# Rotary rows exchanged by transfers inside SBUF instead of products with a permutation matrix

## The reference

```python
def apply_partial_rope(t, cos, sin):
    tf = t.astype(jnp.float32)
    r1, r2 = jnp.split(tf[..., :ROPE_DIM], 2, axis=-1)      # ROPE_DIM = 16
    rot = jnp.concatenate([r1 * cos - r2 * sin, r2 * cos + r1 * sin], axis=-1)
    return jnp.concatenate([rot, tf[..., ROPE_DIM:]], axis=-1).astype(t.dtype)

def dilated_mixer(p, cos, sin):
    q, k, v = [to_heads(t) for t in jnp.split(p, 3, axis=-1)]
    q = apply_partial_rope(q, cos, sin)
    k = apply_partial_rope(k, cos, sin)
    return from_heads(dilated_attention(q, k, v))
```

## Time and profile before

| | us |
|---|---|
| median of 3 runs | 1382.37 (1382.21 to 1382.7) |
| span of the profiled execution | 1380.2 |
| around the span, by the median | 2.2 |
| PE busy | 1368.8, 99% |
| DVE busy | 945.3, 68% |
| ACT busy | 603.8, 44% |
| POOL busy | 119.2, 9% |

### The profile page before, as it was taken

How to read it: one execution, slowest core, us unless ns; L and a number is a source line. 1 busy time by engine, 2 the same in 40 slices (tenths; PEclk the granted TensorE clock), 3 DMA queues, 4 the chain that set the end, 5 groups by cost and what they waited for, 6 DMA issues and landing times.

```text
span 1380.2 us, 18336 instructions
## 1 busy us (share of the span) xinstructions
PE 1368.8 (99%) x6960; PEld 1135.2 (82%) x6960; DVE 945.3 (68%) x1296; ACT 603.8 (44%) x837; POOL 119.2 (9%) x136
## 2 busy tenths in 40 slices
PE   9999999999999999999999999999999999999998
PEld 7777787888788888888888888877888899989986
DVE  7757788545666755763676676767778689548944
ACT  6545687333444533431343544533244345325532
POOL 1010157000000000000000221024000000000000
PEclk9999999999999999999999999999999999999999
DMA  7232345421122332223222323341232242332221
GB/s 268 83 108 77 108 145 198 162 93 61 62 69 87 118 122 92 92 91 114 100 91 71 112 92 95 112 154 36 74 110 92 93 141 102 102 108 98 99 85 62
DMA packets 28031, 144.14 MB, mean 104 GB/s; under 512 B 3146, under 2 KB 8547, under 8 KB 13368
## 3 DMA queue, kind: packets, MB, share of 16 engines
q1 hardware_dynamic: 24616, 133.71, 28.3%
q0 software_dynamic: 2656, 8.72, 1.8%
q10 hardware_dynamic: 688, 0.73, 0.2%
HBM read 136.84 MB, written 6.30 MB: 104 GB/s over the span
## 4 chain that ended last, share of the span: by engine, by line
PE 94%; DVE 2%; ACT 1%; DMA 1%; issue 1%; SPq 0%; POOL 0%; POOLq 0%; DVEq 0%; ACTq 0%
PE ps L2081 28%; PE ps L2083 28%; PE ps L2082 28%; PE ps L2503 1%; PE ps L2305 1%; PE ps L2318 1%; PE ps L2453 1%; PE ps L2295 1%; PE ps L2344 1%; PE ps L2640 1%; PE ps L2642 1%; PE ps L2646 0%; PE ps L2346 0%; PE ps L2345 0%; DMA f_out<-f_out_dram 0%
## 5 line engine op out<-in xcount | busy, mean ns | idle before, releaser
L2081 PE MATMUL ps<-opA_hi,w_hi 128*128 128x512 f32 (+1 forms) x1008 | 387.4, 384 | 1.0 <-DVE w_lo L1260 0.5
L2083 PE MATMUL ps<-opA_hi,w_lo 128*128 128x512 f32 (+1 forms) x1008 | 380.9, 378 | 0.0
L2082 PE MATMUL ps<-opA_lo,w_hi 128*128 128x512 f32 (+1 forms) x1008 | 380.5, 377 | 0.0
L690 ACT CAST w_hi<-raw 128x2048 fp32r<-128x2048 f32 x111 | 211.5, 1906 | 249.2 <-PE ps L2083 248.8
L1260 DVE TENSOR_TENSOR w_lo<-raw,w_hi 128x2048 fp32r<-128x2048 f32 x112 | 256.7, 2292 | 90.2 <-ACT w_hi L690 88.5
L2081 PE MATMUL ps<-opB_hi,w_hi 128*128 128x512 f32 (+1 forms) x584 | 227.4, 389 | 1.5 <-DVE opB_lo L1296 1.0
L2082 PE MATMUL ps<-opB_lo,w_hi 128*128 128x512 f32 (+1 forms) x584 | 225.6, 386 | 0.0
L2083 PE MATMUL ps<-opB_hi,w_lo 128*128 128x512 f32 (+1 forms) x584 | 225.6, 386 | 0.0
L2081 PEld LDWEIGHTS ps<-opA_hi,w_hi 128*128 128x128 f32 x1008 | 189.8, 188 | 38.3 <-issue 3.0
L2083 PEld LDWEIGHTS ps<-opA_hi,w_lo 128*128 128x128 f32 x1008 | 189.7, 188 | 35.7
L2082 PEld LDWEIGHTS ps<-opA_lo,w_hi 128*128 128x128 f32 x1008 | 189.8, 188 | 35.4 <-issue 1.7
(11 more groups left out here) (440 smaller groups left out, 2007.8 us busy)
## 6 DMA issues: line engine op xcount, KB each, us to landing
raw<-weights_dram SPq DMA_DIRECT2D x113, 1024.0 KB, 4.9
g_dram<-g_stage POOLq DMA_DIRECT2D x8, 512.0 KB, 3.0
h<-x_t_dram SPq DMA_DIRECT2D x7, 512.0 KB, 6.2
g_spec<-g_dram SPq DMA_DIRECT2D x5, 512.0 KB, 3.3
scores<-g_dram SPq DMA_DIRECT2D x3, 512.0 KB, 4.9
out_dram<-h SPq DMA_DIRECT2D x6, 256.0 KB, 2.3
mem_raw<-mem_t_dram POOLq DMA_DIRECT2D x1, 1024.0 KB, 7.9
c_keys<-c_dram POOLq DMA_DIRECT2D x4, 256.0 KB, 3.8
```

Of the source, the lines that this page charges most:

```text
L690: A.copy(w_hi[:, p, :], raw[:, p, :]).then_inc(hi_ready, 1)
L2081: W.matmul(out, w[0], x[0], start=start, stop=False, skip_group_check=mixed)
L2082: W.matmul(out, w[0], x[1], start=False, stop=False, skip_group_check=mixed)
L2083: return W.matmul(out, w[1], x[0], start=False, stop=stop, skip_group_check=mixed)
```

## The change

The four products with `rot` are gone from PE and from the list of jobs. SP issues four transfers per tile instead, each of 8 rows of 2 KB, from `rope_raw` to the exchanged rows of `rope_tmp`; they are put in two groups of eight between the loads of pairs 5, 6 and 7. The other rows of `rope_tmp` are cleared once by GpSimd as its first instruction. The sign is the sum of each row of `rot`, taken by DVE once and multiplied into the sine table, and the factor in the sine product changes its sign. The first product of the sine now reads and writes `rope_tmp`. The new counter uses a semaphore that serves a later load too, hence `X_AGAIN_BASE`; the counter of the clearing likewise raises a later count from 2 to 3.

```diff
-JOBS = ["norm", "mlp0", "gates", "norm_mem", "rot0", "rot1", "mlp1", "rot2", "rot3", "mlp2", "vt0", "vt1", "c_tok", "c_row",
+JOBS = ["norm", "mlp0", "gates", "norm_mem", "mlp1", "mlp2", "vt0", "vt1", "c_tok", "c_row",
         "vt2", "vt3", "pool0", "pool1"]
...
+        rot_sign = at("rot_sign", [P, 1], F32, o); o += 4
...
+        rope_moved, X_AGAIN_BASE, rope_cleared = x_again, 256, nyq_cleared
...
-            load_pairs(2, FIRST["v_mem"])
+            def move_rotary_rows(pair):
+
+                sp.wait_ge(rope_cleared, 1)
+                for n in (2 * pair, 2 * pair + 1):
+                    sp.wait_ge(raw_copied, n + 1)
+                    if pair:
+                        sp.wait_ge(roped, n - 1)
+                    for to_row, from_row in ((0, 8), (8, 0), (64, 72), (72, 64)):
+                        sp.dma_start(rope_tmp[to_row:to_row + 8, n % 2, :], rope_raw[from_row:from_row + 8, n % 2, :]
+                                     ).then_inc(rope_moved, 16)
+
+            load_pairs(2, 6)
+            move_rotary_rows(0)
+            sp.wait_ge(lo_ready, 5)
+            sp.dma_start(raw[:, 0, :], a["weights"][in_dram(6)]).then_inc(raw_in[0], 16)
+            move_rotary_rows(1)
+            sp.wait_ge(lo_ready, 6)
+            sp.dma_start(raw[:, 1, :], a["weights"][in_dram(7)]).then_inc(raw_in[1], 16)
+            load_pairs(8, FIRST["v_mem"])
...
         def _(pool):
+            nc.gpsimd.memset(rope_tmp[:], 0.0).then_inc(rope_cleared, 1)
...
                 if n >= 2:
-                    act.wait_ge(misc_done, JOB[f"rot{n - 2}"] + 1)
+                    act.wait_ge(rope_moved, 128)
                 A.copy(rope_raw[:, n % 2, :], ps[:, IN_BANK[c], :]).then_inc(raw_copied, 1)
...
-                act.wait_ge(nyq_cleared, 2)
+                act.wait_ge(nyq_cleared, 3)
...
             split_pair(3)
+            S.link(V.tensor_reduce(rot_sign[:], rot[:], AX.X, ALU.add))
             dve.wait_ge(rope_sin, 2)
             dve.wait_ge(norm_rstd, 1)
-            S.link(V.tensor_tensor(sin_t[:], sin_t[:], rstd[:], ALU.mult))
+            S.link(V.scalar_tensor_tensor(sin_t[:], sin_t[:], rot_sign[:], rstd[:], ALU.mult, ALU.mult))
...
-                bank, read = job_bank(f"rot{n}")
-                if n >= 2:
-                    dve.wait_ge(roped, n - 1)
-                V.scalar_tensor_tensor(rope_tmp[:, n % 2, :], bank, -0.125 if n % 4 < 2 else 1.0, sin_t[:], ALU.mult,
-                                       ALU.mult).then_inc(read, 1)
-                dve.wait_ge(read, JOB[f"rot{n}"] // 2 + 1)
+                rotated = rope_tmp[:, n % 2, :]
+                dve.wait_ge(rope_moved, 128 * (n // 2 + 1))
+                S.link(V.scalar_tensor_tensor(rotated, rotated, 0.125 if n % 4 < 2 else -1.0, sin_t[:], ALU.mult, ALU.mult))
                 dve.wait_ge(q_read, n + 1)
                 V.tensor_tensor(qk[:, n, :], qk[:, n, :], rope_tmp[:, n % 2, :], ALU.add).then_inc(roped, 1)
...
-            dve.wait_ge(x_again, 64)
+            dve.wait_ge(x_again, X_AGAIN_BASE + 64)
...
-            def rotate(n):
-                out = job_bank(f"rot{n}")
-                pe.wait_ge(raw_copied, n + 1)
-                W.matmul(out, rot[:], rope_raw[:, n % 2, :], start=True, stop=True).then_inc(misc_done, 1)
-
...
             in_chunk(5)
-            rotate(0)
-            rotate(1)
             in_chunk(6)
             mlp(1)
-            rotate(2)
-            rotate(3)
             in_chunk(7)
```

## The result

The changed kernel takes 1386.55 us by the median of five runs (1385.62 to 1389.53), the kernel before 1382.22 (1382.06 to 1382.7). The ratio is 1.0036, with a 95% interval of 1.0025 to 1.0047. A few single executions, of the kernel before too, took 1800 to 7843 us; medians, ranges and counts of runs here leave them out. The profiled execution took 1386.55 with a span of 1384.7, against 1380.2.

What follows compares the result with a forecast made beforehand. The prediction took TensorE (PE), busy 99% of the span, to bound the kernel; span 1380.2 less 3.4 for the removed products, other costs nothing, plus 2.2 around it gave 1379.0 us, 8-in-10 range 1378.2 to 1381.2.

Steps and rivals of the forecast that it cites:

- The removed products: PE, two pairs of products with the permutation taken out at 1.71 us each: 3.42 us won, bounds 3.4 to 3.86.
- The job list: PE's PSUM jobs lose four entries, two per bank; each waits only for earlier readers than before, no cost.
- S2: Time at which the second pair's eight transfers land and DVE can start that pair's sine: 63.8 us.
- the narrowest place: PE's transpose of c_neg for c_row: c_neg ready at 73.1, wanted at 74.5, 1.4 us to spare.
- the four rivals: Late landings 1380.7 us (0.17); serial transfers 1391.5 (0.07, with other large costs); more won 1378.5; start held up 1379.9 (0.06).
- the general sign: In the profile after, the prediction is wrong if PE's waits elsewhere grow; no size given.
- The landings: Last of eight transfers lands at 51.6 us (bounds 49.8 to 53.4) for the first pair, 63.8 for the second.
- The margin of the first pair: Third filter layer's operand: the first sine may start as late as 53.0 us before PE waits.
- the sum: Whole kernel: span 1380.2 less 3.4 is 1376.8, with 2.2 us around it 1379.0 us.
- The start: GpSimd's clearing takes about 1.24 us beside DVE's memset of ones; cost to PE 0 to 0.9 us, taken as 0.
- Rival of the transfers that do not overlap: Each transfer waits for the one before; at 1.7 us each PE loses 12.5 at c_row: 1391.5 us; 0.07 with other large costs.

Runs made afterwards that it cites:

- Either order, DVE's or PE's: Changed kernel with DVE reading the third layer's bank ahead of the sine: 1378.80 us; or with PE doing chunk 8 ahead of the transposes of v: 1379.42 us.
- four transfers: Changed kernel with each transfer taking the rows of both tiles, so four issues instead of eight for a pair of tiles: 1385.86 us.
- the filler: Changed kernel plus 14 unused 128x128 products of ones on PE between the two transposes of v: 1384.25 us.

## Why the prediction was wrong

- **The removed products: right.** 3.42 us by the timeline, 3.47 seen in place, 3.1 to 3.6 by putting them back.
- **The job list: this step failed, and with it the wait that it left out.** The prediction said that "each job now waits only for earlier readers than before. No cost", and it followed PE's waits for the third layer's operand and for c_neg alone. The second transpose waits for the reader of the third layer, as before, and was never held against a DVE moved back by its late sine. The rows were there: PE's weight load at 66.01 behind DVE's read, DVE's 0.65 us ahead of that read. Its own numbers would have given it: S2 = 63.8 and four instructions of the two sine tiles, 2.7 us, put the read at 66.5 and its end at 67.0, where PE wanted to transpose at 66.01 - 3.42 = 62.6. That is a wait of 4.4 us; 5.1 were seen with S2 0.7 later. So c_neg, with 1.4 us to spare, was not the narrowest place. Either order, DVE's or PE's, gives the forecast time: 1378.8 and 1379.4 against 1379.0. None of the four rivals named this wait, only the general sign did, "if its waits elsewhere grow".
- **The landings: right within 0.8 us in the changed kernel's trace, the upper bound too low.** 51.6 and 63.8 forecast, 52.39 and 64.54 seen. But over the profiled executions of all kernels with the load ahead, the first sine starts at 51.94 to 52.39 in five and at 54.07, 54.37 and 55.00 in three; the bound was 53.4. For eight transfers the prediction was right that the issues set the landing: from the first issue to the second pair's sine 6.7 us were forecast and 6.72 seen, with and without the load ahead. A part of that is luck, since the starts stand 0.69 apart and not 0.63, and the last transfer lands within 2.0 us and not 2.3. What it lacked is a second limit, seen with four transfers, where the load just ahead holds the landing back. The 2.0 us that it took from the Trainium skill, DMA: Bandwidth & Descriptors, section Anatomy of one DMA, are given there for transfers issued by GpSimd. These are issued by SP, and from the last issue to the sine they took 2.2 and 2.0 us.
- **The margin of the first pair: right.** PE waits when the sine is later than 53.0, shown by 1.1 us at 54.07 and 1.4 at 54.37. Only that it would be later had not been reckoned with.
- **The clock: missing.** An idle stretch of PE was priced at its own length. Here 5.1 us of idling brought 2.36 more, and 4.2 us with four transfers about 2.0 (from the third layer to the transpose of c_neg it is 19.37 us there, of which 4.20 are the wait and 13.21 the work, as in the kernel before); waits of 1.0 and 2.7 brought none, nor did 2.7 behind the filler. So the sum would have missed even with the wait found: 1379.0 + 4.4 = 1383.4. With the 0.7 by which S2 came later and the 2.36 of the clock it is 1386.5, beside 1386.55 measured.
- **The start: right.** GpSimd's clearing takes 0.95 us from 0.75, where 1.24 was reckoned, and PE's first record is at 1.07 as before. The Trainium skill, SBUF — State Buffer, section SBUF: two separate sides, has GpSimd and some DVE instructions lock each other out; DVE's memset of ones, inside those 0.95 us, took its 0.17 us as before, so for it the trace shows no lock.
- **Rival of the transfers that do not overlap: no.** From the first issue to the sine, 45.24 to 52.39, eight take 7.15 us, with starts 0.7 apart. Even if they had run one after another, that is at most 0.89 us each, under the 1.13 at which the rival begins to cost. The Trainium skill, DMA: Bandwidth & Descriptors, section Issuing engines are not separate DMA queues, says that transfers of all issuers run on the same 16 engines and interleave there. The traces agree in that one issuer's transfers delay another's: the mask, issued by GpSimd, lands after 5.1 to 5.4 us in the three kernels without transfers and after 5.8 to 8.3 in the eight that have them behind the load.

**The scatter.** It follows the landings as far as the runs show it. With the 1 MB load ahead of the transfers the ranges are 1.7 to 5.1 us over seven kernels, and 4.3 with eight transfers ahead of it, for whose second pair PE waits. Without transfers, with four of them ahead of the load, or with the products back, they are 0.8 to 1.6. In the three executions with a late first sine it is the whole burst of pair 5, masks and transfers that runs over: the load of the mask took 7.9 to 8.3 us to land, 5.8 to 7.2 in the five others, and the DMA engines still moved data after 52 us. The kernel with the products back (table by stretches, the last two columns being DMA share and GB/s):

```profile
50.00:52.00 2.00, 2.00 (x8) 1.15 (x7) 0.00 (x0) 1.98 (x2) 0.00 (x0) 1.00 0.39 138
52.00:54.00 2.00, 2.00 (x10) 1.66 (x9) 0.00 (x0) 1.97 (x3) 0.00 (x0) 1.00 0.16 55
```

The changed kernel, whose sine started at 52.39:

```profile
50.00:52.00 2.00, 2.00 (x11) 1.65 (x10) 0.00 (x0) 1.98 (x2) 0.00 (x0) 1.00 0.25 71
52.00:54.00 2.00, 2.00 (x11) 1.65 (x10) 1.57 (x3) 1.97 (x3) 0.00 (x0) 1.00 0.00 0
```

That each long run has such a burst is argued from these. What slows the burst in one execution and not in the next stays open.

## What to carry to other kernels

Work taken off the engine that bounds the kernel moves up every wait of that engine, the unchanged ones too. List each wait of it that follows, also those that are met just in time and show no gap, with the instruction that ends it and what stands ahead of that one in its engine's order. That a trace shows no wait does not mean slack: the slack is how long the other engine idled before it did its part, here 0.65 us. A shared buffer that was always read in time is such a wait. And if somebody waits for a small transfer, put it ahead of a bulk load in the order of the issuing engine: it then waits neither for what the load waits for nor, as the four transfers here did, for the load.

## What the runs showed that I had not expected

- The granted clock of PE fell from 1.00 (the 2.4 GHz level) to 0.50 (1.2 GHz) in an idle stretch of 5.1 us, and again in one of 4.2, and stayed low into the next chunk; the first cost 2.36 us, the second about 2.0. After waits of 1.0 and 2.7 us it had not fallen. The length of the wait does not tell alone what it costs: read in quarters of a microsecond, the clock fell at 66.0 in the changed kernel, 3.3 us after PE's last work, and at 64.1 with four transfers, only 1.8 us after it; it was back at 1.00 by 73.0 and 71.0.
- A transfer of 16 KB inside SBUF takes some 0.62 us to issue on SP and one of 32 KB the same; starts stand 0.7 us apart (eight in 5.60 us, four in 2.94).
- With a load of 1 MB ahead, the last of four transfers landed at most 4.6 us after its issue in the first group (47.3 to 51.94) and 3.9 in the second (59.4 to 63.33); with nothing ahead, in at most 2.5 (57.7 to 60.2). The last of eight landed within 2.0 us in the second group, with the load ahead (62.6 to 64.54) and without (60.4 to 62.33).
